# Four of eight x columns as exchanged 32x32 blocks, their squares summed by GpSimd, VectorE and one product, and the rstd transposes moved into the last column

## The reference

```python
def rmsnorm(x, g):
    y = x * rsqrt(mean(x * x, axis=-1, keepdims=True) + EPS)
    return y * g

h = rmsnorm(x, g_pre_mix)
proj = h @ w_in + b_in              # 1024 -> 2304: aq, ak, av, bq, bk, bv
out = concat(mixer_a(...), mixer_b(...))   # window attention with sinks; chunked attention
x = x + rmsnorm(out @ w_out, g_post_mix)
h = rmsnorm(x, g_pre_mlp)
u = square(relu(h @ w_up))          # 1024 -> 4096
x = x + rmsnorm(u @ w_down, g_post_mlp)
```

## Time and profile before

| | |
|---|---|
| median of 3 runs | 1035.18 us (1034.83 to 1035.95) |
| profiled execution, its own time | 1036.56 us |
| its span in the profile | 1034.3 us |
| PE busy in the span | 1023.8 us (99%) |
| first products start, columns 0 to 7 end | 7.16 us, 45.42 us |

### The profile page before, as it was taken

How to read it: one execution, slowest core, us unless ns; L and a number is a source line. 1 busy time by engine, 2 the same in 40 slices (tenths; PEclk the granted TensorE clock), 3 DMA queues, 4 the chain that set the end, 5 groups by cost and what they waited for, 6 DMA issues and landing times.

```text
span 1034.3 us, 15804 instructions
## 1 busy us (share of the span) xinstructions
PE 1023.8 (99%) x5531; PEld 851.2 (82%) x5531; DVE 765.0 (74%) x1498; ACT 471.2 (46%) x989; POOL 217.6 (21%) x213
## 2 busy tenths in 40 slices
PE   8999999999999999999999999999999999999997
PEld 7899887778777888888888888888888888888886
DVE  3854678866689478888988788786454777778997
ACT  5732355554478477846131221221354444444562
POOL 4100000000000003148675675671100000000000
PEclk9999999999999999999999999999999999999999
DMA  9944442110061475145444434446777733454344
GB/s 212 238 130 120 119 130 64 63 49 22 27 202 65 122 174 153 41 132 214 163 173 162 164 132 153 163 141 215 246 244 238 239 98 96 138 196 142 95 138 168
DMA packets 133007, 149.50 MB, mean 145 GB/s; under 512 B 68136, under 2 KB 83376, under 8 KB 130880
## 3 DMA queue, kind: packets, MB, share of 16 engines
q1 hardware_dynamic: 131856, 148.25, 46.3%
q10 hardware_dynamic: 688, 0.20, 0.1%
q0 software_dynamic: 384, 0.04, 0.1%
HBM read 105.22 MB, written 47.49 MB: 148 GB/s over the span
## 4 chain that ended last, share of the span: by engine, by line
PE 94%; SPq 3%; issue 1%; DVE 1%; ACT 1%; DMA 0%; DVEq 0%; ACTq 0%
PE ps L2218 27%; PE ps L2220 27%; PE ps L2219 27%; PE ps L2431 3%; PE ps L2417 3%; PE ps L2398 2%; SPq L693 1%; PE ps L2342 1%; PE ps L2377 1%; PE ps L2550 1%; PE ps L2552 1%; PE ps L2538 1%; SPq L415 1%; PE ps L2568 0%; SPq L684 0%
## 5 line engine op out<-in xcount | busy, mean ns | idle before, releaser
L2219 PE MATMUL ps<-tm_lo,sm_hi 128*128 128x512 f32 (+1 forms) x450 | 174.6, 388 | 0.0
L2220 PE MATMUL ps<-tm_hi,sm_lo 128*128 128x512 f32 (+1 forms) x450 | 174.6, 388 | 0.0
L2218 PE MATMUL ps<-tm_hi,sm_hi 128*128 128x512 f32 (+1 forms) x450 | 174.6, 388 | 0.0
L2218 PE MATMUL ps<-b_hi,wc_hi 128*128 128x512 f32 x448 | 174.6, 390 | 0.0
L2220 PE MATMUL ps<-b_hi,wc_lo 128*128 128x512 f32 x448 | 174.3, 389 | 0.0
L2219 PE MATMUL ps<-b_lo,wc_hi 128*128 128x512 f32 x448 | 174.3, 389 | 0.0
L1475 ACT ACTIVATE sm_hi<-sm_raw 128x512 fp32r<-128x512 f32 x112 | 70.7, 631 | 162.1 <-DMA sm_raw<-u_matrices 162.1
L2122 DVE TENSOR_TENSOR sm_lo<-sm_raw,sm_hi 128x512 fp32r<-128x512 f32 x112 | 77.5, 692 | 78.4 <-ACT sm_hi L1475 77.7
L2219 PEld LDWEIGHTS ps<-tm_lo,sm_hi 128*128 128x128 f32 x450 | 84.5, 188 | 17.6
L2218 PEld LDWEIGHTS ps<-tm_hi,sm_hi 128*128 128x128 f32 x450 | 84.5, 188 | 17.4
L2218 PEld LDWEIGHTS ps<-b_hi,wc_hi 128*128 128x128 f32 x448 | 84.1, 188 | 17.8 <-DVE wc_lo L1894 0.3
(11 more groups left out here) (256 smaller groups left out, 2057.5 us busy)
## 6 DMA issues: line engine op xcount, KB each, us to landing
u_matrices<-stage SPq DMA_DIRECT2D x112, 256.0 KB, 2.0
sm_raw<-u_matrices SPq DMA_DIRECT2D x112, 256.0 KB, 2.7
up_raw<-in_w_up SPq DMA_DIRECT2D x16, 1024.0 KB, 5.1
w<-in_w_down SPq DMA_DIRECT2D x64, 256.0 KB, 4.2
w_raw<-in_w_in SPq DMA_DIRECT2D x8, 512.0 KB, 3.5
xr<-in_x SPq DMA_DIRECT2D x8, 512.0 KB, 4.8
x_rows<-xr SPq DMA_DIRECT2D x8, 512.0 KB, 5.5
xf<-x_rows SPq DMA_DIRECT2D x8, 512.0 KB, 3.6
```

What stands on the lines that cost most here:

```text
L2218: pe.matmul(out, w_hi_, x_hi_, start=start, stop=False)
L2219: pe.matmul(out, w_hi_, x_lo_, start=False, stop=False)
L2220: return pe.matmul(out, w_lo_, x_hi_, start=False, stop=stop)
```

## The change

Column 4 joins the exchanged ones. The rows of columns 5 to 7 are no longer loaded. Their squares, and column 4's, are taken from the blocks as they landed: ACT squares each whole block tile (128x1024, `square_blocks`), GpSimd adds column 5's and 6's squares to column 4's, DVE sums each run of 32 in that sum and in column 7's squares (two reductions, 1024 to 32 per partition), adds the two, and one product with a 0/1 matrix `sel` (made by GpSimd at the start) sums over the four partition groups and leaves the result in bank 6, from which DVE adds it to the row sums of columns 0 to 3 in four small instructions. ACT squares these rows 512 wide, six after column 2 and two after column 3.

On PE the new product stands after the first six products of column 6, and the eight rstd transposes stand after the first six of column 7. On DVE, columns 6 and 7 are turned one step ahead. The scaling of `bcol` and of `sink` moves behind the first two `tile_scaled`. SP issues all blocks one after the other without a wait between them.

```diff
-SQUARED = ((), (), (), (0, 1, 2, 3), (4, 5, 6), (7, 8, 9, 10, 11), (12, 13, 14, 15), ())
+SQUARED = ((), (), (0, 1, 2, 3, 4, 5), (6, 7), (), (), (), ())
-EXCHANGED = (5, 6, 7)
+EXCHANGED = (4, 5, 6, 7)
-SPLIT_WITH = ((), (1,), (2,), (3,), (4, 5), (6, 7), (), ())
+SPLIT_WITH = ((), (1,), (2,), (3, 4), (5,), (6,), (7,), ())
...
-            load_x(4)
-            load_x_blocks(5)
-            for h in range(2):
-                load_x_rows(h)
-            sp.wait_ge(s_xhi, 1)
-            sp.wait_ge(s_xlo, 1)
-            load_x_blocks(6)
-            sp.wait_ge(s_xt, 2)
-            sp.wait_ge(s_sq, 1)
-            load_x_blocks(7)
+            for k in range(KT):
+                if k in EXCHANGED:
+                    load_x_blocks(k)
+                else:
+                    load_x(k)
+                if k in (1, 3):
+                    load_first_weights(sp, (k + 1) // 2)
...
+            for k in EXCHANGED[1:-1]:
+                pool.wait_ge(s_sq, blocks_squared(k))
+                if k > EXCHANGED[1]:
+                    pool.wait_ge(s_part, k - EXCHANGED[1])
+                nc.gpsimd.tensor_tensor(sq_blocks[0][:], sq_blocks[0][:], squares_of(k)[:], ALU.add).then_inc(s_part, 1)
...
+            def square_blocks(k):
+                act.wait_ge(*blocks_landed(k))
+                n = k - EXCHANGED[0]
+                if n >= 3:
+                    act.wait_ge(s_part, n - 2)
+                nc.scalar.activation(squares_of(k)[:], x_blocks[k][:], ACT.Square).then_inc(s_sq, 1)
...
+                    if k > 4:
+                        square_blocks(k)
                     act.wait_ge(s_xt, column_done(k))
                     nc.scalar.activation(x_hi[:, k], column(k), ACT.Copy, scale=g1[:, k:k + 1]).then_inc(s_xhi, 1)
                 for j in SPLIT_WITH[k]:
                     first_hi(j)
+                if EXCHANGED[0] <= k <= 4:
+                    square_blocks(k)
...
+                    if 5 <= k < KT - 1:
+                        turn_blocks(k + 1)
+                    if k == KT - 1:
+                        dve.wait_ge(s_part, len(EXCHANGED) - 2)
+                        nc.vector.tensor_reduce(out=parts[:, 0], in_=sq_blocks[0][:].rearrange("p (c i) -> p c i", i=32),
+                                                axis=mybir.AxisListType.X, op=ALU.add).then_inc(s_ss1, 1)
+                        dve.wait_ge(s_sq, blocks_squared(k))
+                        nc.vector.tensor_reduce(out=parts[:, 1], in_=squares_of(k)[:].rearrange("p (c i) -> p c i", i=32),
+                                                axis=mybir.AxisListType.X, op=ALU.add).then_inc(s_ss1, 1)
+                        dve.wait_ge(s_ss1, 2)
+                        nc.vector.tensor_tensor(parts[:, 2], parts[:, 0], parts[:, 1], ALU.add).then_inc(s_ss1, 1)
...
-            dve.wait_ge(s_const, 192)
-            nc.vector.tensor_scalar(bcol[:, 1:9], bcol[:, 1:9], -SCALE, None, ALU.mult).then_inc(s_bsc, 1)
-            nc.vector.tensor_scalar(sink, sink, -1.0, None, ALU.mult).then_inc(s_sink, 1)
...
             dve.wait_ge(s_row, 1)
             tile_scaled(0)
             tile_scaled(1)
+            dve.wait_ge(s_const, 192)
+            nc.vector.tensor_scalar(bcol[:, 1:9], bcol[:, 1:9], -SCALE, None, ALU.mult).then_inc(s_bsc, 1)
+            nc.vector.tensor_scalar(sink, sink, -1.0, None, ALU.mult).then_inc(s_sink, 1)
...
+            def add_squares():
+                pe.wait_ge(s_xlo, column_done(EXCHANGED[0] - 1))
+                pe.wait_ge(s_id, 9)
+                pe.wait_ge(s_ss1, 3)
+                pe.matmul(ps[:, 6, 0:32], sel[:], parts[:, 2], start=True, stop=True).then_inc(s_ss1, 1)
...
+                    if e == 2 and k == KT - 2:
+                        add_squares()
+                    elif e == 2 and k == KT - 1:
+                        row_transposes()
```

More of the change, by code:

```diff
@@ L208, in column_done, with rows_squared, blocks_squared @@
     return 2 * (k + 1) if k < 2 else k + 3
+def rows_squared(k):
+    return sum(len(SQUARED[j]) for j in range(k))
+ROW_SQUARED = [n + 1 + max(0, k - EXCHANGED[0] + 1) for k in range(KT) for n in SQUARED[k]]
+def blocks_squared(k):
+    return rows_squared(k) + k - EXCHANGED[0] + 1
 def chunks_until(n):
@@ L310, in build @@
         sq = sb("sq", 150.25, [P, 2, KX, P])
+        sel = sb("sel", 154.25, [P, P])
+        parts = sb("parts", 154.75, [P, 3, 32])
+        sq_blocks = [sb(f"sq_blocks{n}", at, [P, SEQ]) for n, at in enumerate((155.25, 122, 188 if KX == 3 else 184))]
         wv_hi = [sb(f"wv_hi{k}", at, [P, VW], F32R) for k, at in enumerate((84, 86.5, 89, 91.5, 94, 96.5, 116, 118.5))]
@@ L314, in build @@
                          for n, dt in (("wv_raw", F32), ("wv_lo", F32R)))
-        x_blocks = {k: sb(f"x_blocks{k}", at, [P, SEQ]) for k, at in zip(EXCHANGED, (92, 76, 108))}
-        x_turned = {k: sb(f"x_turned{k}", at, [P, SEQ]) for k, at in zip(EXCHANGED, (112, 116, 76))}
+        x_blocks = {k: sb(f"x_blocks{k}", at, [P, SEQ]) for k, at in zip(EXCHANGED, (188, 92, 76, 108))}
+        x_turned = {k: sb(f"x_turned{k}", at, [P, SEQ]) for k, at in zip(EXCHANGED, (192, 112, 116, 76))}
         bv_cols = sb("bv_cols", 121, [P, 32])
@@ L963, in _ @@
             nc.gpsimd.memset(bv_cols[:], 0.0).then_inc(s_id, 1)
+            nc.gpsimd.memset(sel[:], 0.0).then_inc(s_id, 1)
+            for a in range(4):
+                pool.wait_ge(s_id, 5 + a)
+                nc.gpsimd.affine_select(out=sel[:].rearrange("p (b i) -> p b i", i=32), in_=sel[:].rearrange("p (b i) -> p b i", i=32),
+                                        compare_op=ALU.not_equal, fill=1.0, base=-32 * a, pattern=[[0, 4], [-1, 32]],
+                                        channel_multiplier=1).then_inc(s_id, 1)
             pool.wait_ge(s_xt, 2)
@@ L1137, in tile_hi @@
                                      bias=bias_of(e)).then_inc(s_ehi, 1)
-            for k in range(2):
-                value_hi(k)
             act.wait_ge(s_rowp, 1)
@@ L1527, in first_lo, with turn_blocks @@
                                         ).then_inc(s_w1lo, 1)
+            def turn_blocks(k):
+                dve.wait_ge(*blocks_landed(k))
+                if k == KT - 1:
+                    dve.wait_ge(s_sq, blocks_squared(k - 1))
+                    dve.wait_ge(s_xt, column_done(k - 1))
+                nc.vector.transpose(x_turned[k][:], x_blocks[k][:]).then_inc(s_xt, 1)
             dve.wait_ge(s_g1, 16)
@@ L1544, in _ @@
                                                    ).then_inc(s_xlo, 1)
-                    if k < EXCHANGED[0]:
+                    if k <= EXCHANGED[0]:
                         first_lo(k)
-                if k + 1 in EXCHANGED:
-                    dve.wait_ge(*blocks_landed(k + 1))
-                    nc.vector.transpose(x_turned[k + 1][:], x_blocks[k + 1][:]).then_inc(s_xt, 1)
-                    first_lo(k + 1)
                 if k == 5:
@@ L1553, in _ @@
                     nc.vector.transpose(bv_rows[:], bv_cols[:]).then_inc(s_bv, 1)
-                elif k == KT - 2:
-                    dve.wait_ge(s_sq, 2 * T)
-                    nc.vector.tensor_tensor(ss1, ss1, ya1, ALU.add).then_inc(s_ss1, 1)
+                elif k == KT - 1:
+                    dve.wait_ge(s_ss1, 4)
+                    for q in range(4):
+                        rows = slice(32 * q, 32 * q + 32)
+                        last = nc.vector.tensor_tensor(ss1[rows], ss1[rows], ps[rows, 6, 0:32].rearrange("p (t q) -> p q t", q=4)[:, q],
+                                                       ALU.add)
+                    last.then_inc(s_ss1, 1)
+                    first_lo(k)
                     dve.wait_ge(s_std1, 1)
@@ L2233, in x_transposes, with row_transposes @@
                 last.then_inc(s_xt, 1)
+            def add_squares():
[3 more added lines that the diff above has]
+                pe.matmul(ps[:, 6, 0:32], sel[:], parts[:, 2], start=True, stop=True).then_inc(s_ss1, 1)
+            def row_transposes():
+                pe.wait_ge(s_rcol, 2)
+                for t in range(T):
+                    last = pe.transpose(two(6)[:, t * P:(t + 1) * P], rcols[:, t * P:(t + 1) * P], ident[:])
+                last.then_inc(s_rowp, 1)
             def first_products(k):
@@ L2285, in _ @@
                     x_transposes(k + 1)
-                elif k == KT - 1:
-                    pe.wait_ge(s_xlo, column_done(EXCHANGED[0] - 1))
-                    pe.wait_ge(s_rcol, 2)
-                    for t in range(T):
-                        last = pe.transpose(two(6)[:, t * P:(t + 1) * P], rcols[:, t * P:(t + 1) * P], ident[:])
-                    last.then_inc(s_rowp, 1)
                 first_products(k)
```

58 lines of the change are left out of this document (23 added, 35 removed).

## The result

| | before | after |
|---|---|---|
| median (lowest to highest), 6 runs each | 1035.39 us (1034.83 to 1036.14) | 1039.67 us (1038.06 to 1040.32) |
| profiled execution, its span | 1036.56 us, 1034.3 us | 1039.38 us, 1037.6 us |
| mean granted clock of that execution | 0.999 | 0.997 |

The ratio is 1.0038, 95% interval 1.0025 to 1.0051: the change makes the kernel slower by about 4 us, beyond the 0.2% that a measurement can tell. On the scale of the 1035.18 us of the prediction the ratio gives 1039.1. The forecast was 1037.1 with a range from 1034.6 to 1039.5, and its likeliest case was "within 0.2%". The time went the way that was forecast and lies inside the range, close to its upper end; the rise is twice the forecast, and the likeliest case was the wrong one.

The account below looks back on a forecast made before the run. PE's stream and its few waits were taken to bound the kernel (busy 1023.8 of 1034.3 us). Terms -0.79 - 0.57 + 1.51 + 0.5 + 1.24 = +1.89 us gave 1037.1 us, range 1034.6 to 1039.5.

Parts of the forecast that it names:

- within 0.2%: Whole kernel: the time differs from before by too little for a measurement to tell; chance 0.56.
- Column 4's transposes: PE's front: eight transposes before column 4's products go away, -0.79 us.
- the wait before column 6: PE's front: the wait for column 6's late blocks goes if blocks arrive in time, -0.57 us.
- Column 5's wait: PE before column 5's products: waits for x_lo, behind column 6's turning and slowed by GpSimd, +1.51 us, bounds 0 and +5.05.
- The product with sel: PE after six products of column 6: short wait for DVE's reductions plus the product itself, +0.5 us, bounds 0.1 and 2.5.
- What I counted at nothing: ACT's squares, GpSimd's bias loads and SP's attention bias loads: hidden behind other work, 0 us.
- The value products: PE before column 6's value products: wv_lo late through the moved scaling of bcol, +1.24 us, bounds 0.9 and 1.7.
- Late blocks: Rival at the front: blocks at 117 GB/s or with two pauses, column 6 landing at 30 to 31, 1039.3 us; chance 0.20.
- In time: Rival at the front: column 6 lands by 27.5, additions miss x_lo, +0.1 to +0.9 us, 1035.7 us; chance 0.18.
- the third rival: Value products: their wait stays away because DVE reaches the scaling 1.2 us earlier, -1.2 us, 1034.0 us; chance 0.10.
- the pause of 1.5 us: Block transfers: one slow stretch like the earlier window 21 to 22, counted into column 6's landing at 28.5.
- The estimate of 249 GB/s: Block transfers: rate from the skill's fixed descriptor cost, 2.1 us a column, column 6 before 27; not followed.

Follow-up runs that it names:

- e1: Changed kernel with GpSimd's two additions cut to 32 of 1024 columns, most squares of columns 5 and 6 left out: 1036.0 us, ratio 1.0003.
- e4: Changed kernel with column 5 turned into PSUM instead of SBUF and its low weight part made ahead of that turning: 1037.56 us, ratio 1.0018.
- e8: Changed kernel with column 5 turned into PSUM, weight parts made earlier, scaling of bcol ahead of both tmp, two wv_hi earlier: 1034.94 us, ratio 0.9994.
- e9: Kernel of e8 with column 7's high weight part made later on ACT, and two products with sel replacing DVE's small addition: 1035.05 us, ratio 0.9996.
- e10: Kernel of e9 with GpSimd's two additions cut to 32 of 1024 columns: 1035.06 us, ratio 0.9995.
- e5: Kernel before the change plus two GpSimd additions of 128x1024 that nothing reads: 1036.24 us, ratio 1.0009.
- e11: Kernel before the change plus two GpSimd additions of 128x512 with two different inputs, which nothing reads: 1035.04 us, ratio 0.9996.
- e7: Changed kernel, front alone reordered: column 5 turned into PSUM, weight parts of columns 5 to 7 made earlier: 1036.7 us, ratio 1.0011.
- e2: Changed kernel with the scaling of bcol and of the sinks back ahead of the first two tmp: 1039.03 us, ratio 1.0031.
- e3_pe_awake: Changed kernel with twenty unread identity transposes on PE ahead of column 5's products, filling its wait: 1038.21 us, ratio 1.0023.
- e6: Changed kernel with the scaling of bcol back ahead of both tmp and wv_hi of columns 2 and 3 made earlier: 1038.4 us, ratio 1.0024.

## Why the prediction was right or wrong

The time lies inside the range, but in part by luck: the upper end was drawn for late blocks, and the blocks came early. Of the terms, three held and one was too large; column 5's wait was too small, and the clock was not in the sum at all.

**Column 4's transposes (-0.79) and the wait before column 6 (-0.57).** Both as forecast: -0.77, and no wait there.

**Column 5's wait (+1.51, became +2.39).** This is the step that failed. The prediction put `x_lo` of column 5 right behind the turning of column 6, and that right behind the landing: 28.5 + 1.24 + 2.31. The landing was later in my sum than in fact (27.0 in e1; 27.1 to 27.7 in e4, e8, e9 and e10, where DVE waited for it too), so by those prices DVE would have been through at 30.6, and PE, free at 25.50 + 4.15 = 29.65, would have waited 0.9 us. But the first addition had no victim in my sum. I named two additions and priced one meeting. The first meets w_lo of column 5, which stands ahead of the turning of column 6 on DVE: 2.34 us instead of 0.52, so the turning began at 28.14 and not at the landing. And the second cost x_lo 1.50 us (2.74 against 1.24 in e1), not 1.03. I had taken as a price for the size of the instruction (128x1024: 2.31); what decides is how much of the addition is still to come when the instruction starts. Six meetings show it, and so do the two rows themselves, once GpSimd's rows are laid beside them:

```profile
406.32 1.74 POOL L1036 TENSOR_TENSOR wc_raw<-up_raw,wc_raw 128x512 f32<-128x512 f32 x1
408.01 2.26 POOL L1028 TENSOR_TENSOR wc_raw<-up_raw 128x512 f32<-128x512 f32 x1
...
498.20 1.75 POOL L1033 TENSOR_TENSOR wc_raw<-up_raw 128x512 f32<-128x512 f32 x1
```


| DVE instruction | alone | GpSimd's instruction still to come at its start | lost |
|---|---|---|---|
| after, w_lo of column 5 | 0.52 | 1.92 | 1.82 |
| after, x_lo of column 5 | 1.24 | 1.66 | 1.50 |
| e4, w_lo of column 6 | 0.52 | 2.13 | 2.02 |
| e8, x_lo of column 6 | 1.24 | 0.75 | 0.59 |
| e5, x_lo of column 5 | 1.28 | 1.89 (all) | 1.74 |
| e11, x_lo of column 5 | 1.28 | 1.29 (all) | 1.14 |
| before, b_lo at 406.82 | 1.23 (at 366.22) | 1.24 | 1.08 |
| before, wc_lo at 498.72 | 0.68 | 1.23 | 1.10 |

Four meetings more are in the text or agree with it: e7's x_lo of column 6 (1.23 to come, 1.07 lost), e5's w_lo of column 4 (0.74 and 0.61), and e2's two, which repeat the changed kernel's.

The rule of the Trainium skill that I had set beside it (GPSIMD Engine Reference, "Specifications") is borne out on both sides: two SBUF inputs are held up, the turning with its one input kept 1.24 though the addition began 0.44 us into it (28.14) and 1.25 wholly inside one (e8), and an x_lo that reads PSUM kept 1.28 (e5, e11).

**The clock (not in the sum, +1.52).** The prediction let PE wait and resume at full speed. e3_pe_awake shows that the wait itself cost this: with PE busy through the same wait, column 5's products took 4.21 us instead of 5.67.

**The product with sel (+0.5, became about 0.2).** There was no wait, since PE itself came 2.4 us late. Column 6's piece took 4.35 us, 0.2 over the rule. In e1, where column 5 was in time, it took 4.47, so that DVE's chain shows there by some 0.1 us.

**What I counted at nothing.** It cost nothing that shows: column 6's products to the value products took 9.32 us against 9.37.

**The value products (+1.24, became +1.21, and 0.34 in small waits and restarts beside it).** Right in mechanism and nearly in size: ACT waited for the scaling of `bcol` 2.51 us; e2, with the scaling alone put back, left 0.62 of the 1.21, and e6, which also makes two `wv_hi` earlier, left nothing. The sum behind it was off by 0.05: its terms give R + 6.05, not R + 6.10, and so +1.19.

**The rivals.** "Late blocks" named 1039.3, close to what came, for a reason that did not occur: the sixteen issues took 13.58 us, and the blocks were early. "In time" is what e1 measured once the additions were away. The value wait of the third rival came, so that rival did not. The blocks came as the earlier trace rows had it, without the pause of 1.5 us that I had added: 17.5 + 3 x 3.1 is 26.8, which is also what the lower bound, given as 27.2, should have been. The estimate of 249 GB/s that I had worked out from the Trainium skill (DMA: Bandwidth & Descriptors, "Why small descriptors are slow (HBM only)") did not come about: 154 GB/s over the 13.58 us of issue, with windows of 1 us up to 211 between 17 and 28. Whether SP's issuing or the packets set this rate, no run here separates.

**What stays open.** Why some executions of the changed kernel seem to keep the clock and others don't. e6 has the same two groups (1036.65 to 1036.77 with a mean clock of 0.998 to 1.0; 1038.15 to 1040.05 with 0.995 to 0.997), e3 with its filler does not. In e2 the mean clock does not tell the two lowest times (1036.92 and 1037.40, both 0.998) from the others, and single executions up to 1037.4 us occur in e9, e10 and the kernel before as well, at 0.997 to 0.999, so not every such difference is the clock. And whether e8 is truly faster than the kernel before, which its interval leaves open by 0.03%.
